# FFN gate and up: both parts of the input moved as 512 columns, halves added on VectorE

## The reference, cut to what matters

```python
D_MODEL = 1024; SEQ = 256; D_FF = 2816; DEPTH_2 = 4

def swiglu(x, w_gu, w_down):                  # in short
    g, u = split(x @ w_gu)                    # 1024 -> 2 x 2816
    return (silu(g) * u) @ w_down             # 2816 -> 1024

for layer in range(DEPTH_2):
    h = x + 0.5 * swiglu(rmsnorm_2(x, g[0]), w_ffn_gu[layer, 0], w_ffn_down[layer, 0])
    h = h + mixer(rmsnorm_2(h, g[1]))
    h = h + 0.5 * swiglu(rmsnorm_2(h, g[2]), w_ffn_gu[layer, 1], w_ffn_down[layer, 1])
    x = h + sigmoid(rmsnorm_2(h, g[3]) @ w_ple_gate[layer]) * (p[layer] @ w_ple_proj[layer])
```

## Time and profile before

| | |
|---|---|
| median of 3 runs | 2852.26 us (2850.64 to 2853.08) |
| profiled execution, its own time | 2852.43 us |
| its span, first to last instruction | 2850.2 us |
| TensorE busy | 2645.0 us (93%) |
| VectorE busy | 1787.7 us (63%) |
| ScalarE busy | 1309.1 us (46%) |
| mean granted TensorE clock | 0.969 |
| FFN tile in the steady state | 8.61 us |
| weights read | 414 MB, mean 146 GB/s |

### The profile page before, as it was taken

How to read it: one execution, slowest core, us unless ns; L and a number is a source line. 1 busy time by engine, 2 the same in 40 slices (tenths; PEclk the granted TensorE clock), 3 DMA queues, 4 the chain that set the end, 5 groups by cost and what they waited for, 6 DMA issues and landing times.

```text
span 2850.2 us, 52656 instructions
## 1 busy us (share of the span) xinstructions
PE 2645.0 (93%) x20946; PEld 2589.3 (91%) x20946; DVE 1787.7 (63%) x2494; ACT 1309.1 (46%) x1932; POOL 105.9 (4%) x109
## 2 busy tenths in 40 slices
PE   6878888799998999999889999996999999999998
PEld 5878878799988999999789999995999999988998
DVE  5575675656676667655566576565656755686656
ACT  3554463544525445444354454454544544525444
POOL 0010002000020000000000000000000000020000
PEclk8999999899999999999999999998999999999999
DMA  5221330355533555554435545551455455533553
GB/s 188 99 82 60 104 111 23 110 192 177 178 112 104 192 177 170 178 184 141 143 110 195 185 166 178 184 177 38 148 184 181 159 183 185 172 103 106 195 185 113
DMA packets 113940, 418.38 MB, mean 147 GB/s; under 512 B 12672, under 2 KB 12800, under 8 KB 113280
## 3 DMA queue, kind: packets, MB, share of 16 engines
q1 hardware_dynamic: 113088, 413.10, 42.7%
q0 software_dynamic: 560, 2.10, 0.2%
q10 hardware_dynamic: 144, 1.05, 0.1%
HBM read 414.10 MB, written 2.10 MB: 146 GB/s over the span
## 4 chain that ended last, share of the span: by engine, by line
PE 82%; DVE 10%; ACT 5%; issue 2%; DMA 0%; POOL 0%; SPq 0%; ACTq 0%; DVEq 0%
PE ps_gu L138 16%; PE ps_gu L144 15%; PE ps_gu L139 15%; PE ps_acc L138 7%; PE ps_acc L139 7%; PE ps_acc L144 7%; DVE w_lo L98 2%; PE ps_acc L1854 1%; PE ps_acc L153 1%; PE ps_acc L158 1%; PE ps_acc L154 1%; PE ps_acc L2244 1%; PE ps_acc L1106 1%; PE ps_acc L1888 1%; ACT w_hi L90 1%
## 5 line engine op out<-in xcount | busy, mean ns | idle before, releaser
L98 DVE TENSOR_TENSOR w_lo<-w_raw,w_hi 128x1024 fp32r<-128x1024 f32 x781 | 953.6, 1226 | 496.3 <-ACT w_hi L90 496.2
L138 PE MATMUL ps_gu<-xn_hi,w_hi 128*128 128x256 f32 x4000 | 1140.4, 288 | 74.0 <-DVE w_lo L98 28.2
L139 PE MATMUL ps_gu<-xn_hi,w_lo 128*128 128x256 f32 x4000 | 1133.1, 286 | 0.0
L144 PE MATMUL ps_gu<-xn_lo,w_hi 128*128 128x256 f32 x4000 | 1081.0, 284 | 0.0
L90 ACT ACTIVATE w_hi<-w_raw 128x1024 fp32r<-128x1024 f32 x781 | 819.6, 1055 | 501.6 <-PE ps_gu L144 333.4
L138 PEld LDWEIGHTS ps_gu<-xn_hi,w_hi 128*128 128x128 f32 x4000 | 780.1, 195 | 81.4 <-DVE w_lo L98 39.8
L139 PEld LDWEIGHTS ps_gu<-xn_hi,w_lo 128*128 128x128 f32 x4000 | 780.1, 195 | 0.3
L144 PEld LDWEIGHTS ps_gu<-xn_lo,w_hi 128*128 128x128 f32 x4000 | 745.7, 193 | 0.0
L138 PE MATMUL ps_acc<-h_hi,w_hi 128*128 128x256 f32 x1496 | 422.6, 282 | 1.4 <-DVE h_lo L471 1.4
L139 PE MATMUL ps_acc<-h_hi,w_lo 128*128 128x256 f32 x1496 | 421.1, 281 | 0.0
L144 PE MATMUL ps_acc<-h_lo,w_hi 128*128 128x256 f32 x1496 | 420.8, 281 | 0.0
(11 more groups left out here) (382 smaller groups left out, 2783.5 us busy)
## 6 DMA issues: line engine op xcount, KB each, us to landing
w_raw<-in_w_dram SPq DMA_DIRECT2D x781, 512.0 KB, 3.9
const<-in_const_dram SPq DMA_DIRECT2D x1, 1280.0 KB, 8.9
x_res<-in_x_dram SPq DMA_DIRECT2D x1, 1024.0 KB, 4.9
distance_rows<-arena POOLq DMA_DIRECT2D x1, 1024.0 KB, 4.8
p_all<-distance_rows POOLq DMA_DIRECT2D x2, 512.0 KB, 4.8
p_all<-in_p_dram ACTq DMA_DIRECT2D x1, 1024.0 KB, 4.8
out_dram<-x_res SPq DMA_DIRECT2D x1, 1024.0 KB, 3.8
vec<-in_vec_dram SPq DMA_DIRECT2D x1, 170.0 KB, 4.9
```

The costliest lines, as they stand in the source:

```text
L98: dve.tensor_tensor(self.w_lo[:, s, :], self.w_raw[:, c % NR, :], self.w_hi[:, s, :], ALU.subtract)\
L138: pe.matmul(out, self.w_hi[:, s, j0:j0 + width], rhs_hi, start=start, stop=False, skip_group_check=True)
L139: pe.matmul(out, self.w_lo[:, s, j0:j0 + width], rhs_hi, start=False, stop=False, skip_group_check=True)
L144: return pe.matmul(out, self.w_hi[:, s, j0:j0 + width], rhs_lo, start=False, stop=last, skip_group_check=True)
```

## The change

The high and the low part of the input lie side by side in one buffer (`xn_parts`, 512 columns for each block of 128 inputs: 256 of x_hi, 256 of x_lo). For tiles 1 to 21 gate and up use `with_both`: one matmul of w_hi over all 512 columns, and one of w_lo over the 256 of x_hi. The product with x_lo lands in columns 256 to 511 of the bank, so gate and up now take a bank each, and two tiles in turn take four banks: the two old ones and `ps_sum` and `ps_misc`. Tile 0 keeps its three matmuls of 256 columns in the same new layout. ScalarE copies the second halves of both banks to SBUF (`low`), VectorE adds them to the first halves, and then the old chain runs. During an FFN the normalizer uses bank 0 of `ps_acc`. Waits on the readers of the side banks are added where these are now written.

```diff
+    def with_both(self, pe, out, s, j0, width, rhs, first, last):
+        pe.matmul(out, self.w_hi[:, s, j0:j0 + width], rhs, start=first, stop=False, skip_group_check=True)
+        return pe.matmul(out[:, 0:S], self.w_lo[:, s, j0:j0 + width], rhs[:, 0:S], start=False, stop=last,
+                         skip_group_check=True)
...
 def sum_squares(k, pe, n=None):
+    pe.wait_ge(*k.side_read[0])
...
-            mm = pe.matmul(k.ps_sum[:, tt:tt + 1], ...
+            mm = pe.matmul(k.ps_norm[:, tt:tt + 1], ...
...
 def ffn(k):
+    low = k.arena.buf[:, 0:2 * S].rearrange("p (n t) -> p n t", n=2)
+    k.ps_norm = k.ps_acc[:, 0, :]
...
+    def bank(t, n):
+        return k.ps_four[:, 2 * (t % 2) + n, :]
...
         def first():
-            pe.wait_ge(*free[0])
             for n in range(2):
+                pe.wait_ge(*free[n])
                 k.wait_chunk(pe, c0 + n)
...
             if t == 1:
-                pe.wait_ge(*free[1])
+                pe.wait_ge(*side_free[0])
+                pe.wait_ge(*side_free[1])
+                pe.wait_ge(*k("misc_free").made())
...
-                    mm = k.products(pe, k.ps_gu[t % 2][:, n * S:(n + 1) * S], c % NS, j * P, P,
-                                    k.xn_hi[:, j, :], k.xn_lo[:, j, :], False, j == KD - 1,
-                                    start=(n == 0 and j == 0))
+                    mm = k.with_both(pe, bank(t, n), c % NS, j * P, P, k.xn_parts[:, j, :], j == 0, j == KD - 1)
...
     def _(act):
+            act.wait_ge(k.chunk_done.sem, g + 2 + i * TURN)
+            if t:
+                act.wait_ge(*added.at(b0 + t + STEP * i))
+            act.activation(low[:, :, :], k.ps_four[:, 2 * (t % 2):2 * (t % 2) + 2, S:2 * S], ACT.Copy).then_inc(lows.sem, 1)
...
     def _(dve):
-            dve.wait_ge(k.chunk_done.sem, g + 2 + i * TURN)
-            gu = k.ps_gu[t % 2][:, :].rearrange("p (n t) -> p n t", n=2)
+            gu = k.ps_four[:, 2 * (t % 2):2 * (t % 2) + 2, 0:S]
+            dve.wait_ge(*lows.at(b0 + t + 1 + STEP * i))
+            dve.tensor_tensor(gu, gu, low[:, :, :], ALU.add).then_inc(added.sem, 1)
+            dve.wait_ge(*added.at(b0 + t + 1 + STEP * i))
             dve.tensor_tensor(gu, gu, k.rstd[:, :].unsqueeze(1).to_broadcast([P, 2, S]), ALU.mult).then_inc(sc.sem, 1)
...
 def setup(nc, ctx, io, n_chunks, n_vec, n_const=1):
-    k.xh = [k.sb(f"xn_hi{b}", [P, KD, S], F32R) for b in range(2)]
-    k.xl = [k.sb(f"xn_lo{b}", [P, KD, S], F32R) for b in range(2)]
+    k.xx = [k.sb(f"xn_parts{b}", [P, KD, 2 * S], F32R) for b in range(2)]
+    k.xh = [xx[:, :, 0:S] for xx in k.xx]
+    k.xl = [xx[:, :, S:2 * S] for xx in k.xx]
...
+    k.ps_four = ctx.enter_context(nc.psum_tensor("ps_four", [P, 4, 2 * S], F32))
+    k.ps_gu = [k.ps_four[:, i, :] for i in range(2)]
+    k.ps_sum, k.ps_misc = k.ps_four[:, 2, :], k.ps_four[:, 3, :]
```

More of the change, by code:

```diff
@@ L111, in take @@
         self.read_until[self.cur] = self.used
-        self.cur, self.xn_hi, self.xn_lo = b, self.xh[b], self.xl[b]
+        self.cur, self.xn_hi, self.xn_lo, self.xn_parts = b, self.xh[b], self.xl[b], self.xx[b]
         self.xn_hi_at = [self("xn_hi_ready").at(h0 + j // per + 1) for j in range(KD)]
@@ L306, in sum_squares @@
         for tt in range(TT):
-            mm = pe.matmul(k.ps_sum[:, tt:tt + 1], k.xn[:, m, tt * P:(tt + 1) * P], k.ones[:, 0:1],
+            mm = pe.matmul(k.ps_norm[:, tt:tt + 1], k.xn[:, m, tt * P:(tt + 1) * P], k.ones[:, 0:1],
                            start=(m == 0 and tt == 0), stop=(m == 1), skip_group_check=True)
@@ L347, in take_rstd @@
     dve.wait_ge(*k("rstd_rows").at(n))
-    dve.tensor_copy(k.rstd[:, :], k.ps_sum[:, 0:S]).then_inc(k("rstd_ready").sem, 1)
+    dve.tensor_copy(k.rstd[:, :], k.ps_norm[:, 0:S]).then_inc(k("rstd_ready").sem, 1)
 def ffn(k):
@@ L356, in ffn @@
     b0 = silu.n
-    free, hi_at, lo_at = k.gu_read, k.xn_hi_at, k.xn_lo_at
+    added, lows = k("gu_added"), k("gu_low_copied")
+    low = k.arena.buf[:, 0:2 * S].rearrange("p (n t) -> p n t", n=2)
+    free, side_free, hi_at, lo_at = k.gu_read, k.side_read, k.xn_hi_at, k.xn_lo_at
+    k.ps_norm = k.ps_acc[:, 0, :]
     LOOPS = (FT - 6) // STEP
@@ L391, in first @@
         def first():
-            halves = [k.ps_gu[0][:, n * S:(n + 1) * S] for n in range(2)]
-            pe.wait_ge(*free[0])
             for n in range(2):
+                pe.wait_ge(*free[n])
                 k.wait_chunk(pe, c0 + n)
@@ L399, in first @@
                 for n in range(2):
-                    k.with_hi(pe, halves[n], (c0 + n) % NS, j * P, P, k.xn_hi[:, j, :], n == 0 and j == 0)
+                    k.with_hi(pe, bank(0, n)[:, 0:S], (c0 + n) % NS, j * P, P, k.xn_hi[:, j, :], j == 0)
             for j in range(KD):
@@ L403, in first @@
                 for n in range(2):
-                    mm = k.with_lo(pe, halves[n], (c0 + n) % NS, j * P, P, k.xn_lo[:, j, :], j == KD - 1)
+                    mm = k.with_lo(pe, bank(0, n)[:, S:2 * S], (c0 + n) % NS, j * P, P, k.xn_lo[:, j, :],
+                                   j == KD - 1)
                     if j == KD - 1:
@@ L440, in tile @@
                 act.wait_ge(*hr.at(b0 + t - 1 + STEP * i))
-            act.activation(k.s[:, t % 2, :], k.ps_gu[t % 2][:, 0:S], ACT.Silu).then_inc(silu.sem, 1)
+            act.activation(k.s[:, t % 2, :], bank(t, 0)[:, 0:S], ACT.Silu).then_inc(silu.sem, 1)
             if 1 <= t < FT - 1:
@@ L465, in tile @@
                 dve.wait_ge(*hl.at(b0 + t - 1 + STEP * i))
-            dve.tensor_tensor(k.h[:, t % 2, :], k.s[:, t % 2, :], k.ps_gu[t % 2][:, S:2 * S], ALU.mult)\
+            dve.tensor_tensor(k.h[:, t % 2, :], k.s[:, t % 2, :], bank(t, 1)[:, 0:S], ALU.mult)\
                .then_inc(hr.sem, 1)
@@ L476, in ffn @@
     spread_root(k)
-    for s in (silu, hr, hh, hl, sc):
+    k.ps_norm = k.ps_sum
+    for s in (silu, hr, hh, hl, sc, added, lows):
         s.n += FT
@@ L481, in ffn @@
     k.late = ([k.used - 1 + AHEAD], [k.used - 2 + AHEAD, k.used - 1 + AHEAD])
-    k.gu_read, k.slot = [hr.made()] * 2, 0
+    k.gu_read, k.side_read, k.slot, k.side_bank = [hr.made()] * 2, [hr.made()] * 2, 0, 0
     residual(k, 0.5)
@@ L533, in ple @@
     xn_hi, xn_lo = k.xn_hi, k.xn_lo
-    free = k.gu_read
+    free, side_free = k.gu_read, k.side_read[1]
     gc = lambda m: c0 + 2 + m
@@ L571, in _ @@
             k.wait_chunk(pe, gc(m))
-            pe.wait_ge(*(gate.at(g0 + m - 2) if m > 2 else k("misc_free").made()))
+            pe.wait_ge(*(gate.at(g0 + m - 2) if m > 2 else side_free))
             for j in range(KD):
```

11 lines of the change are left out of this document (3 added, 8 removed).

## The result

The changed kernel takes 2869.68 us (median; 2866.97 to 2870.19), the kernel before 2851.45 us (2849.91 to 2853.08): a ratio of 1.0062, 95% interval 1.0044 to 1.0079. It is slower by some 18 us, where 9 us faster was forecast. The time lies outside the range given. The profiled execution took 2866.97 us, its span is 2865.1 us (before: 2850.2).

A forecast was written before the change was run, and what follows sets the result against it. TensorE was taken as the bound, with gate/up/down paid per matmul. 35.8 - 6.7 - 10.8 - 3.3 - 1.8 - 4.2 = 9.0 us gained, giving 2843 us; range 2833 to 2859, the main case's own 2838 to 2849.

The forecast's parts named there:

- Part 1: Gate/up, tiles 1 to 21: a 512- and a 256-column matmul replace three of 256, saving 13.3 ns per group, 35.8 us gained.
- the first rival: At the 2688 groups, the narrow matmul takes the saving back: 2861 us at half the saving, 2879 at none; chance 0.13.
- Part 2: Copy and add in steady-state tiles: each chain grows by 1.36 us, hidden by 3.3 us of cover; cost 0.
- Parts 3 and 4: Longer chain at each FFN's ends: first tile loses 6.7 us, last tile 10.8 us, over 8 FFNs.
- Part 5: Tile 0 waits for two banks: 3.3 us at PLE seams, 1.8 after output projections, 4.2 from the lower clock.
- The fixed part of 2.5 ns: Rival: one matmul less saves only 2.5 ns, so the gain is 6.7 us and the time 2872; chance 0.04.
- seams or ends would be cheap: Rival: clock stays up at PLE seams or ends hide half the added chain; losses about 17 us, time 2834; chance 0.13.
- the loop's chain would bind: Rival: a tile's chain or VectorE becomes the loop's bound; 0.1 us beyond the cover is 17 us, time 2860; chance 0.05.
- The sign of being wrong: The prediction is wrong if the loop's tile is 8.55 us or more, or if the waits at either end are absent.

The follow-up runs named there:

- experiment 3: Changed kernel, but the w_lo matmul also moves all 512 columns, which adds the product w_lo*x_lo; 3140.11 us (one run).
- experiment 4: Changed kernel with its banks, waits, copy and add, but three 256-column matmuls again in place of the wide and narrow pair; 2881.35 us, ratio 1.0110.
- experiment 2: Changed kernel, but in each chunk the 8 matmuls of 512 columns come first, then the 8 of 256; 2850.13 us, ratio 0.9998.
- 10: Changed kernel with its matmuls in the order wide, wide, narrow, narrow over two input blocks; 2852.72 us, ratio 1.0004.
- 11: Changed kernel with tiles 0 and 21 in the old form, and tiles 1 to 20 in the order wide, wide, narrow, narrow; 2822.18 us, ratio 0.9898.
- 12: Changed kernel with tiles 0 and 21 in the old form, and tiles 1 to 20 with four wide, then four narrow matmuls; 2834.38 us, ratio 0.9940.
- 1: Changed kernel, but the narrow matmul (w_lo*x_hi) adds into columns 256 to 511, the other half of the bank; 2869.83 us, ratio 1.0069.
- 7: Changed kernel with tiles 0 and 21 in the old form: three 256-column matmuls, one bank, no copy and add, old wait; 2838.03 us, ratio 0.9953.
- experiment 5: Kernel before the change, with only tile 0's wait for the readers of both banks taken over; 2870.2 us, ratio 1.0066.
- 6: Changed kernel with tile 0 alone in the old form: one bank, no copy and add, old wait; 2847.24 us, ratio 0.9983.
- 8: Changed kernel with tiles 0 and 21 in the old form, and each chunk's wide matmuls first in tiles 1 to 20; 2833.48 us, ratio 0.9933.
- 9: Kernel of experiment 2, but all 8 wide matmuls of a chunk move the same block of x, block 0; 2852.41 us (one run).

## Why the prediction was wrong, step by step

**Part 1 is the step that failed: the price of the pair.** It put the pair at 226.7 + 120.0 = 346.7 ns, "since both pure streams show the same 13.3 ns". Both widths are right in a pure stream (experiments 3 and 4). The sum of two pure streams is not the price of an alternating one: 353.6 ns. The saving is 6.4 ns a pair in place of 13.3. A tile saves 0.111 us, a little more than 16 x 6.4 ns, since its 24 matmuls of down take 2.847 us in place of 2.853; over the run that is 18.6 us in place of 35.8. This alone turns the sign: the first rival had put the turning point at 10.0 ns. It named the narrow matmul as the place; by the rows the excess is at the wide one (236.6 against 226.7), while the narrow one is even cheaper (117.0). Experiments 2 and 10 to 12 show the cause to be the order of widths, with the half of the bank that the narrow one adds to (1) and the joined input, its blocks and the turns of w_hi and w_lo (3) ruled out; what in TensorE makes it so is open.

"No row has a 256-column matmul behind a 512-column one" was not so. The trace of the kernel before passes from one width to the other in its mixers. Timeline, TensorE, the start and the end of such a stream of 96 wide ones:

```profile
787.13 0.28 PE L144 MATMUL ps_gu<-xn_lo,w_hi 128*128 128x256 f32 x1
787.25 0.40 PE L153 MATMUL ps_acc<-w_hi,xn_hi 128*128 128x512 f32 x1
787.48 0.40 PE L154 MATMUL ps_acc<-w_lo,xn_hi 128*128 128x512 f32 x1
787.72 0.39 PE L158 MATMUL ps_acc<-w_hi,xn_lo 128*128 128x512 f32 x1
...
809.04 0.28 PE L138 MATMUL ps_gu<-xn_hi,w_hi 128*128 128x256 f32 x1
809.15 0.28 PE L139 MATMUL ps_gu<-xn_hi,w_lo 128*128 128x256 f32 x1
```

The first five wide ones take 233, 236, 228, 233 and 230 ns and only then 227; the first narrow one behind the stream takes 113. Rows 4 lie inside such a stream, where the price has settled, and in the changed kernel it never settles. These rows do not give 353.6, but they show that the price of a matmul depends on what ran before it, so that the pair was an open price and not a sum.

The Trainium skill (TensorE: Matmul & The Clock Gate, "Back-to-back issue gap") gives a rule by which I estimate a pair at 512/2.4 + 256/2.4 + 5 = 325.0 ns; no order here came within 23 ns of that.

**Part 2 held.** 0 was forecast; the chain grew by 1.36 us to 5.06, as said, and the tile of experiment 4 is that of before. The cover was 3.28 us (1257.30 to 1260.58), where 3.3 was forecast.

**Parts 3 and 4 held.** Forecast 0.84 + 1.35 = 2.19 us per FFN, measured 0.77 + 1.37 = 2.14 in the changed kernel and 2.08 in experiment 4. Removing both made every FFN shorter (7).

**Part 5 had the right places and was too low.** A PLE seam was forecast at 1.1 + 1.4 = 2.5 us. Two of them cost 2.7 us; the one shown above, at the lower clock for 6.8 us where the others had 3.4, cost 3.6. After an output projection 0.6 was forecast and 1.0 measured: 0.16 of it because TensorE starts 0.22 us after the recorded end of the add, not 0.06, the rest is not cut further. Together 12.2 against 9.3. What was missing altogether is the time outside the FFNs, 4.2 us. In before, one of four idle stretches of 2.48 us between an FFN and PLE is followed by clock 0.50; in the changed kernel and in experiment 5 all four are, at about 1.5 us each. In experiment 5 nothing near them was edited; they start at another time. That the time of start decides it fits, but no run changed that alone. The forecast allowed 3 us for this in its own range, and no direction.

**The sum.** 9.0 us gained was forecast. Part 1 gave 17.2 less, seams and clock took 7.1 more, the ends 0.4 less: 9.0 - 17.2 - 7.1 + 0.4 = -14.9, the difference of the spans. The medians lie 18.2 us apart; the profiled execution was the fastest of the changed kernel's four.

**The rivals.** The first (saving taken back, 2861 at half of it) is what happened, with 7 us of seams and clock on top. The fixed part of 2.5 ns came closest in time, 2872, but that is luck: 6.4 ns were saved, and 11.2 in the best order; its gain was 12 us too small and its losses 7 us too small. That seams or ends would be cheap, or the loop's chain would bind, both fell.

**The sign of being wrong was set too wide.** The prediction called itself wrong from a loop tile of 8.55 us on. The tile came out at 8.50 and the kernel is slower all the same: with 26.8 us of losses over 168 loop tiles the change breaks even at 8.607 - 0.160 = 8.45 us.

## What to carry to other kernels

Price a mix of matmul widths from a mix, not from two pure streams; where the trace has none, look at the first matmuls behind a change of width, take the price as open, and try the order (here 353.2 to 348.4 ns a pair for the same work). Compare such kernels by the stage that was edited: two orders differed by 19.5 us in time and by 9.5 in the FFNs. A saving of a few ns per matmul in a loop is soon eaten by fixed costs at its ends: here 2.1 us at the two ends of each FFN and 1.0 to 3.6 us at the seams of six of the eight, so keep the old form in the first and the last tile and let only the covered ones change. A second bank for the first tile means a second reader to wait for: ask what frees it.

## What the runs showed of the hardware

- Distances between matmul starts are uneven where widths alternate: the changed kernel repeats 232, 118, 240, 120, 236, 113 ns (means by place in the tile), two by two 233, 234, 115, 115, 233, 233, 114, 117. Behind narrow ones the first wide ones vary from 224 to 236 ns before they settle at 227: the first nine of a tile in experiment 3, all eight of gate and the first five of up in experiment 2, the first five in the mixer stream above. The narrow ones settle at 120.
- Whether TensorE's idle 2.48 us between an FFN and PLE are followed by 1.2 GHz differed between kernels with the same instructions around them: 1 of 4 in before, 4 of 4 in the changed kernel and experiments 1 and 5, 3 in 6, 7 and 12, 2 in 4, 8, 10 and 11, 1 in 2 and 9. Each costs about 1.5 us. With what the lower clock costs in other places, kernels that differ only inside the FFNs lie up to some 9 us apart outside them (experiments 8 and 11).
